# Gate columns moved from the channel-major tiles to the token-major products of a hybrid decoder layer

## The reference

```
h = rmsnorm(x); proj = h @ w_in
u, z, xbc, dt_raw, qk, v, i_raw, f_raw, o_raw = split(proj)      # 512,768,1280,12,768,768,6,6,768
y_a = s5(u):    diagonal complex state space, 32 groups x 16 channels, state 64,
                then g = gelu(y); y_a = g * sigmoid(g @ w_glu + b_glu)
y_b = ssd(z, silu(causal_conv(xbc)), softplus(dt_raw + bias)):  12 heads, gated by silu(z), norm
y_c = mlstm(silu(causal_conv(qk)), v, i_raw + b_i, log_sigmoid(f_raw + b_f)): 6 heads, * sigmoid(o_raw)
x = x + rmsnorm(concat(y_a, y_b, y_c) @ w_out)
x = x + rmsnorm((silu(h2 @ w_gate) * (h2 @ w_up)) @ w_down)      # h2 = rmsnorm(x)
```

## Time and profile before

| | before |
|---|---|
| median of 3 runs | 2898.15 us (2896.5 to 2898.3) |
| profiled execution, its own time | 2895.86 us |
| its span, mean granted clock of TensorE | 2894.0 us, 0.994 |
| PE busy | 2846.0 us (98%) |
| DVE, ACT, POOL busy | 66%, 41%, 13% |
| the 640 + 640 + 640 matmuls of L1900 | 387, 371, 370 ns mean (they overlap) |
| idle of PE before L1900, and what ended most | 5.1 us, DVE t_w_lo L1761 4.3 |
| chain that ended last | PE 47%, DVE 2%, DMA 1%, ACT 1% |

### The profile page before, as it was taken

One profiled execution on the slowest core, in us unless ns is written; L12 is line 12 of the kernel. 1 busy time (PEld: TensorE's weight loads), 2 busy tenths in 40 slices (PEclk: granted clock), 3 DMA queues, 4 the chain that ended last, 5 costly groups with the idle time before them and its releaser, 6 DMA issues.

```text
span 2894.0 us, 36039 instructions
## 1 busy us (share of the span) xinstructions
PE 2846.0 (98%) x13576; PEld 2304.7 (80%) x13576; DVE 1903.5 (66%) x2616; ACT 1191.6 (41%) x2005; POOL 386.0 (13%) x496
## 2 busy tenths in 40 slices
PE   8999999999999989999999999999999999999998
PEld 5888888777777767888888788888888888888887
DVE  7677887666853358887343776666866655656656
ACT  6222222454443445545333533333533333545543
POOL 0000000012530236664121100000000000000000
PEclk9999999999999999999999999999999999999999
DMA  4222443446665958887878654444542223866862
GB/s 162 73 73 86 135 132 112 145 143 203 222 198 159 299 173 279 278 300 272 303 268 332 239 197 164 168 153 165 172 172 94 106 98 138 333 194 210 285 195 103
DMA packets 294569, 545.14 MB, mean 188 GB/s; under 512 B 59228, under 2 KB 150780, under 8 KB 284924
## 3 DMA queue, kind: packets, MB, share of 16 engines
q1 hardware_dynamic: 262636, 437.69, 45.2%
q0 software_dynamic: 24704, 75.52, 6.9%
q10 hardware_dynamic: 7056, 29.63, 2.6%
HBM read 358.30 MB, written 184.44 MB: 188 GB/s over the span
## 4 chain that ended last, share of the span: by engine, by line
PE 47%; DVE 2%; DMA 1%; ACT 1%; issue 1%; SPq 0%; DVEq 0%; ACTq 0%
PE f_banks L2985 25%; PE f_banks L2993 14%; PE f_banks L2087 7%; DMA f_h_raw<-hq 1%; PE f_banks L2290 0%; DMA f_bop2lo<-hq 0%; DVE f_snap L2788 0%; DVE f_w_op L2762 0%; DVE f_a L2800 0%; ACT f_w_op L2624 0%; DVE f_a L2795 0%; ACT o_late L2191 0%; ACT f_snap L2642 0%; DVE f_raw L2776 0%; DVE f_bop2lo L2755 0%
## 5 line engine op out<-in xcount | busy, mean ns | idle before, releaser
L2993 PE MATMUL f_banks<-f_d_op 128*128 128x512 f32 x1848 | 419.0, 389 | 0.0
L2993 PEld LDWEIGHTS f_banks<-f_d_op 128*128 128x128 f32 x1848 | 347.1, 188 | 71.8
L2832 DVE TENSOR_TENSOR f_d_op<-f_d_raw,f_d_op 128x1024 fp32r<-128x1024 f32 x154 | 187.4, 1225 | 149.0 <-ACT f_d_op L2663 148.4
L674 PE MATMUL t_banks<-h_hi,c_w_hi 128*128 128x512 f32 x640 | 254.5, 398 | 0.0
L1900 PE MATMUL t_banks<-t_w_hi,h_hi 128*128 128x512 f32 (+1 forms) x640 | 247.9, 387 | 5.1 <-DVE t_w_lo L1761 4.3
L674 PE MATMUL t_banks<-h_hi,c_w_lo 128*128 128x512 f32 x640 | 250.0, 391 | 0.0
L674 PE MATMUL t_banks<-h_lo,c_w_hi 128*128 128x512 f32 x640 | 249.3, 389 | 0.0
L2663 ACT ACTIVATE f_d_op<-f_d_raw 128x1024 fp32r<-128x1024 f32 x154 | 162.8, 1061 | 198.3 <-PE f_banks L2993 161.5
L1900 PE MATMUL t_banks<-t_w_lo,h_hi 128*128 128x512 f32 (+1 forms) x640 | 237.7, 371 | 0.0
L1900 PE MATMUL t_banks<-t_w_hi,h_lo 128*128 128x512 f32 (+1 forms) x640 | 236.8, 370 | 0.0
L2642 ACT ACTIVATE f_snap<-f_banks 128x1024 f32<-128x1024 f32 x88 | 90.3, 1026 | 253.6 <-PE f_banks L2985 253.6
(11 more groups left out here) (410 smaller groups left out, 6293.3 us busy)
## 6 DMA issues: line engine op xcount, KB each, us to landing
f_raw<-in_w_gu SPq DMA_DIRECT2D x88, 512.0 KB, 6.3
sop<-f_a SPq DMA_DIRECT2D x154, 256.0 KB, 2.0
f_d_raw<-sop SPq DMA_DIRECT2D x154, 256.0 KB, 2.9
t_raw<-in_w_tok SPq DMA_DIRECT2D x72, 512.0 KB, 4.6
f_d_raw<-top SPq DMA_DIRECT2D x88, 256.0 KB, 4.4
m_bc<-rows SPq DMA_DIRECT2D x16, 1152.0 KB, 6.8
f_d_raw<-in_w_dn SPq DMA_DIRECT2D x66, 256.0 KB, 3.1
o_y_lo<-y_lo SPq DMA_DIRECT2D x16, 1024.0 KB, 7.8
```

The lines of the kernel that those rows point to most:

```text
L674: last = nc.tensor.matmul(banks[:, p % RING, :], w[:, n % 2, k, :], h[:, q, k, :], start=k == 0 and j == 0, stop=k == KD - 1 and j == 2)
L2832: tt(d_op[d % D_RING][:, 2:4], d_raw[:, d % S_RING], d_op[d % D_RING][:, 0:2].bitcast(F32), sub).then_inc(dlo_ok, 1)
L2993: last = nc.tensor.matmul(banks[:, bank, :], d_op[d % D_RING][:, s, tok], d_op[d % D_RING][:, w, :], start=k == 0 and j == 0, stop=k == FU ...
```

## The change

- Channel stage: the gate tile is gone (20 tiles, 4 pieces fewer); the convolved tiles begin one tile earlier against the work on S5's constants. ACT does the sines and cosines of that work ahead of an evacuation, not behind it. Tile 8 of the convolved ones (NOT_TOK) is no longer stored token-major: 4 pieces of 4 transposes fewer, and narrower loads in the mixers. Two semaphores become one.
- L707's products alternate between the two lanes, in the order q, r, g. In the S5 steps the input products (L1932) change their loops from lane, r to r, lane.
- Token stage: the 24 gate columns stand ahead of v, z and o; the 2328 columns go in five groups of 466 (the last 464), each of two units with 4 of the 8 depth tiles. The first group (gate columns and 442 of v) is made for all four blocks before the others, with weights that are loaded and split once. 160 slots of 12 matmuls. The weight splits are 68 of 932 columns, before 72 of 1024. One narrow group of each block now begins with 162 columns of Silu and ends with 304 of Sigmoid; another is Copy 326, Silu 140.
- The first 16 evacuations also copy the gate columns to gate_cols; PE transposes them to rows in PSUM (gate_transposes), which DVE's gate work reads. DVE clears gate_cols in the last channel tile.
- POOL sends 7 pieces of a tile per block, before 6. The slots of gates, S5, GLU and mixers are later by 4 to 20, in a list that is longer by 16.

```diff
-    GATE, FIRST = UT, UT + 1
+    FIRST = UT
...
-                evac(n, q)
                 if n == 2 and q == 0:
                     trigonometry()
+                evac(n, q)
...
-                for g in range(2):
-                    lanes = slice(g * S5P, (g + 1) * S5P)
-                    for q in range(2):
-                        for r, b_in in enumerate((bbr, bbi)):
+                for q in range(2):
+                    for r, b_in in enumerate((bbr, bbi)):
+                        for g in range(2):
+                            lanes = slice(g * S5P, (g + 1) * S5P)
...
-    AHEAD, AHEAD_MASK, AHEAD_EXP, AHEAD_W, AHEAD_1 = 112, 129, 132, 116, 140
+    AHEAD, AHEAD_MASK, AHEAD_EXP, AHEAD_W, AHEAD_1 = 132, 148, 151, 136, 156
...
-    WIDTH = (NB, NB, NB, NB, NB // 2)
-    PARTS = (((ACT.Silu, 0, 0, NB),),
-             ((ACT.Silu, 0, NB, NB // 2), (ACT.Copy, NB // 2, XW + VW + NB, NB // 2)),
-             ((ACT.Copy, 0, XW + VW, NB),),
-             ((ACT.Sigmoid, 0, XW, NB),),
-             ((ACT.Sigmoid, 0, XW + NB, NB // 2),))
-    GATE_SLOT, GATE_STEP, COLS = 6, 11, (8, 6, 6, 8)
-    S5_SLOT, S5_STEP = 52, 2
-    GLU_SLOT, GLU_STEP = 90, 14
+    WIDTH = (WT, WT, WT, WT, XW + 2 * VW + GATES_T - 4 * WT)
+    V_AT = XW + VW
+    V0 = WT - GATES_T
+    Z0 = WT - (VW - V0)
+    Z1 = Z0 + WT
+    O0 = WT - (XW - Z1)
+    PARTS = (((ACT.Copy, GATES_T, V_AT, V0),),
+             ((ACT.Copy, 0, V_AT + V0, VW - V0), (ACT.Silu, VW - V0, 0, Z0)),
+             ((ACT.Silu, 0, Z0, WT),),
+             ((ACT.Silu, 0, Z1, XW - Z1), (ACT.Sigmoid, XW - Z1, XW, O0)),
+             ((ACT.Sigmoid, 0, XW + O0, VW - O0),))
+    GATE_SLOT, GATE_STEP, COLS = 10, 12, (8, 6, 6, 8)
+    ROWS_SLOT, ROWS_STEP = 9, 8
+    S5_SLOT, S5_STEP = 61, 2
+    GLU_SLOT, GLU_STEP = 99, 14
...
+                if e < QT * BLK:
+                    nc.scalar.activation(gate_cols[:, e, 0:HS], banks[:, e % QT, 0:HS], ACT.Copy)
+                    nc.scalar.activation(gate_cols[:, e, FR:GCW].rearrange("p (g r) -> p g r", g=2)[:, :, 0:HM],
+                                         banks[:, e % QT, HS:GATES_T].rearrange("p (g r) -> p g r", g=2), ACT.Copy)
...
+                    nc.vector.memset(gate_cols, 0.0)
...
-            b, i = divmod(unit, UNITS_T)
-            return (b * GROUPS_T + i // 2) if i % 2 or i == UNITS_T - 1 else None
+        def group_of(n):
+            return (n, 0) if n < BLK else ((n - BLK) // (GROUPS_T - 1), 1 + (n - BLK) % (GROUPS_T - 1))
+        def weights_of(step_):
+            return step_ % 2 if step_ < 2 * BLK else step_ - 2 * BLK + 2
...
+            def gate_transposes(c):
+                if c == 0:
+                    pe.wait_ge(const_in, 80)
+                    banks_read(pe)
+                pe.wait_ge(evac_ok, QT * (c + 1))
+                if c >= 2:
+                    pe.wait_ge(args_ok, c - 1)
+                for a in range(QT):
+                    last = nc.tensor.transpose(row_banks[c % 2][:, a * P:(a + 1) * P], gate_cols[:, QT * c + a, 0:RG], ident_sb[:])
+                last.then_inc(rows_mm, 1)
...
-                for e in range(2):
-                    lanes = slice(e * S5P, (e + 1) * S5P)
-                    for r in range(2):
+                for r in range(2):
+                    for e in range(2):
+                        lanes = slice(e * S5P, (e + 1) * S5P)
...
-        halves = [w[half, :, :, n * NB:(n + 1) * NB] for n in range(4) for half in range(2)]
-        rest = w[:, :, :, 4 * NB:].reshape(KD, P, NB // 2)
-        return np.stack([unit.transpose(1, 0, 2).reshape(P, -1) for unit in halves + [rest]])
+        w = np.concatenate([w, np.zeros((D, 5 * WT - w.shape[1]), np.float32)], 1)
+        w = w.reshape(2, KD // 2, P, 5, WT)
+        return w.transpose(3, 0, 2, 1, 4).reshape(10, P, KD // 2 * WT)
```

More of the change, by code:

```diff
@@ L1470, in split_at, with row_step @@
         def split_at(slot):
-            unit, t = divmod(slot, 4)
-            both = 4 * unit in range(GATE_SLOT, GATE_SLOT + GATE_STEP * BLK, GATE_STEP)
-            if t > 1 or unit + 1 == UNITS:
-                return ()
-            return (() if t else (0, 1)) if both else (t,)
+            step_, t = divmod(slot, 4)
+            follows = step_ + 1 < STEPS_T and (step_ == 0 or step_ + 1 >= 2 * BLK)
+            return ((weights_of(step_ + 1), t),) if t < 2 and follows else ()
+        def row_step(slot):
+            c, r = divmod(slot - ROWS_SLOT, ROWS_STEP)
+            return c if r == 0 and 0 <= c < BLK else None
         def glu_step(slot):
@@ L1502, in tiles_sent @@
             for b in range(2):
[L1503 removed]
+                eng.wait_ge(out_sent[b], 16 * sends(TILES_T * BLK - TILES_LAST * (BLK - blocks) + b))
         def glu_done(eng):
@@ L1529, in load @@
                     tok_stored(sp)
-                sp.dma_start(raw[half][:], w_tok[unit % UNITS_T, :, half * 2 * NB:(half + 1) * 2 * NB]).then_inc(raw_in[half], 16)
+                sp.dma_start(raw[half][:, 0:2 * WT], w_tok[unit if unit < 2 else 2 + (unit - 2) % W_UNITS, :, half * 2 * WT:(half + 1) * 2 * WT]
+                             ).then_inc(raw_in[half], 16)
             def ahead(q):
@@ L1587, in _ @@
             c_sync(sp, ahead)
-            for unit in range(UNITS):
+            for unit in range(STEPS_T):
                 for t in range(4):
-                    if t < 2 and unit + 2 < UNITS:
-                        load(unit + 2, t)
+                    if t < 2 and unit == 0:
+                        load(2, t)
+                    elif t < 2 and 2 * BLK < unit + 2 < STEPS_T:
+                        load(weights_of(unit + 2), t)
                     slot = 4 * unit + t
@@ L1639, in send_s5 @@
                                    ys[j * S5H:(j + 1) * S5H]).then_inc(y_sent, 16)
-            for unit in range(UNITS):
-                n = group(unit)
+            for unit in range(STEPS_T):
                 for t in range(4):
-                    if n is not None:
-                        send(QT * n + t)
+                    if unit % 2:
+                        send(QT * (unit // 2) + t)
                     q = s5_step(4 * unit + t)
@@ L1665, in upper @@
                     convolved(act, 2 + 2 * unit)
-                nc.scalar.activation(w_hi[unit % 2][half][:], raw[half][:], ACT.Copy).then_inc(whi_ok, 1)
+                nc.scalar.activation(w_hi[unit % 2][half][:, 0:2 * WT], raw[half][:, 0:2 * WT], ACT.Copy).then_inc(whi_ok, 1)
             def ahead(q):
@@ L1730, in _ @@
             c_scalar(act, ahead)
-            for unit in range(UNITS):
-                n = group(unit)
+            for unit in range(STEPS_T):
                 for t in range(4):
                     slot = 4 * unit + t
-                    for half in split_at(slot):
-                        upper(unit + 1, half)
-                    if n is not None:
-                        evac(QT * n + t)
+                    for part in split_at(slot):
+                        upper(*part)
+                    if unit % 2:
+                        evac(QT * (unit // 2) + t)
                     gates(slot)
@@ L1865, in _ @@
             c_vector(dve, ahead)
-            for unit in range(UNITS):
+            for unit in range(STEPS_T):
                 for t in range(4):
                     slot = 4 * unit + t
-                    for half in split_at(slot):
-                        lower(unit + 1, half)
+                    for part in split_at(slot):
+                        lower(*part)
                     gates(slot)
@@ L1967, in _ @@
                     products(unit, t)
+                    c = row_step(slot)
+                    if c is not None:
+                        gate_transposes(c)
                     gates(slot)
```

146 lines of the change are left out of this document (77 added, 69 removed).

## The result

| | before | after |
|---|---|---|
| median | 2896.5 us (5 runs, 2894.96 to 2898.3) | 2911.3 us (5 runs, 2909.05 to 2914.39) |
| profiled span | 2894.0 us | 2907.3 us |
| ratio after/before | | 1.0051, 95% interval 1.0036 to 1.0065 |

The change makes the kernel slower by about 15 us. The forecast was 2893, 5 us faster, with a range of 2870 to 2914: the time lies inside the range, on the other side of no change. A second measurement beside other runs on another chip gives 1.0048 (1.0032 to 1.0064).

A forecast was written before the change was run, and what follows sets the result against it. PE's own columns were taken to set the time (PE 98% busy), other engines showing only where PE stops. Terms from -21.8 to +9 summed to -4.6 us, giving 2893 us, with an 8-in-10 range of 2870 to 2914.

The forecast's parts named there:

- Gate tile, lanes, transposes, channel stall: Channel stage: gate tile -21.8, L707's lanes paired -3.5, tile 8's transposes gone -1.9, PE waiting before first transposes +6.9 us.
- Products: Token-major matmuls: 1920 of 466 or 464 columns, about 207 ns each by a straight line, cost +4.0 us.
- Gates' phase: Token stage: weights split once leave the gates' chains nearly free in early slots, so PE's stalls shrink, -5 us.
- S5 steps: Token stage: PE's work between steps shrinks below DVE's recurrence, so PE waits in each of 15 steps, +3.8 us.
- Group of Silu and Sigmoid: Last block: two table loads a tile make ACT late for a lower, and POOL's mask delays sends, +9 us.
- GLU entry: First GLU product waits for the last g by DMA while the slots before it are shorter, +1.5 us.
- R2: Rival: ACT's tables bind in all four blocks, +21 us, 2914; chance 0.22.
- R3: Rival: 466 columns cost as much as 512, +41.6 in place of +4.0, 2931; chance 0.04.
- R1: Rival: the waits don't come in channel stage, recurrence or ACT's tables; 2867; chance 0.12.
- R4: Rival: L1932 gains too and the gates' stalls go fully, -8 and -5 more, 2880; chance 0.06.
- The drain behind a table load: Skill page's 1.38 us drain beside each 1.28 load, making the two-function group dearer in every block; some 2927; chance 0.02.

The follow-up runs named there:

- e5: Changed kernel with the split weights laid 512 columns apart in place of 466, products still 466 wide: 2909.88 us, 1.0048 against before.
- e3: Changed kernel with S5_SLOT 62 in place of 61, so the S5 steps stand at even slots as before: 2898.55 us, 1.0004 against before.
- e4: Changed kernel with SP's loads for the later S5 steps issued ahead of their slot's weight loads, first two steps' unmoved: 2901.35 us, 1.0012 against before.
- e10: Changed kernel with all S5 loads ahead of their slot's weights, the first two steps' ahead of those of slots 56 and 57: 2901.01 us, 1.0014 against before.
- e1: Changed kernel with Silu in place of Sigmoid in the two-function group, so part of the result differs: 2901.91 us, 1.0013 against before.
- e2: Changed kernel with columns reordered so that no group has both Silu and Sigmoid: 2900.21 us, 1.0009 against before.
- e6: Changed kernel with WT 512: four groups of 512 columns and one of 280 per block: 2943.83 us, 1.0164 against before.

## Why the prediction was wrong

- *Gate tile, lanes, transposes, channel stall*: forecast -20.3 together (-21.8, -3.5, -1.9, +6.9), measured -20.0. (In the other profiles with the same lane order the token stage begins at 508.1 to 510.1, so that number is good to about 1.) Each showed where it was said: stall 5.1, lane groups 0.98, the input products unchanged. Right. One reading in it was wrong and harmless: the window 189.43 to 213.55 holds no L707; four transposes take 0.35 to 0.53 to the next matmul all the same.
- *Products, +4.0*: mis-sized. The spacing of 512 columns was read in the channel stage, 226.7; in the token stage it was 11.02/48 = 229.6 already before, and 466 are 10.16/48 = 211.7, not 207.3. By these spacings the 1920 products take 407 against 398: +8 to +9, where the forecast had +4.0. Most of the rest of the 11.6 is half clock behind the new stalls. e5 shows that alignment isn't the cause. Why the token stage is 3 ns a matmul dearer was not looked into.
- *Gates' phase, -5*: PE's waits there went from 5.9 to 2.6 us, and the half clock after the 3.43 stall is gone. Right in kind and roughly in size.
- *S5 steps, +3.8*: this is the step that failed. It priced DVE's recurrence, and that came about as said (2.1 in thirteen waits). It took the recurrence for all that a step waits for, and left out the loads that SP issues: they are in no sentence of the working. PE's waits for u went from 1.1 to 13.0 us, so the step's waits cost 14.0 more in place of 3.8, with half clock behind them. The move from slot 52 to 61 puts the steps at odd slots, where two weight loads stand ahead of every other step's loads: 6.6, which e3 and e4 take away. The first step's wait, 1.06 before and in no term, became 6.4, and e10 takes it away by the place in the queue alone. That ACT's tables are what makes the queue late there is shown for the issue of the loads (e1, e2) and not for the whole wait. The order of SP's program would have shown the two weight loads.
- *Group of Silu and Sigmoid, +9*: the mechanism is right (two loads a tile, each 1.28), the stall is 4.0, at the lower end of the bounds; the mask did delay sends, but ACT waited only 0.58 and 0.74 for them. What was missed is the same group in the first block, where it delays an upper, the lower behind it and so SP's loads ahead of the first S5 step. Without the double loads the kernel is 10 to 11 us faster (e1, e2), so the term's size of 9 comes near, but by luck: it is not one stall in the last block.
- *GLU entry, +1.5*: measured +1.3 in the profile (1.95 for 0.65); in the other kernels with 466 columns the wait is 1.1 to 3.9.
- *The time*: 2911 lies in the range because the range was wide; the forecast's direction was wrong, 5 faster against 15 slower.
- *Rivals*: R2 (tables bind in more than the last block; 2914) was the nearest: time 2911. But that is luck. It named each block's fourth group as the place; blocks two and three have no such stall, and the first paid through SP. R3 falls (466 columns take 18 ns less than 512). R1 and R4 fall. The drain behind a table load, which the Trainium skill gives ("ScalarE: Activation LUTs", "What ACT_TABLE_LOAD costs"), isn't in these rows either: the load at 659.60 ends at 660.88, and the next activation starts at 660.89. The working's 2927 for it doesn't follow from its own terms: 4 x 8 + 6 over 2893 is 2931.

## What to carry to other kernels

When slots move, walk every queue past the new places, DMA issuers first: a load costs what stands ahead of it, and here an odd slot for an even one was 7 us of waits (7.1 to 0.8 in e3). Don't let one evacuation need two function tables; put a copied range between them in the layout (e2: 11 us). And keep slots equal where the same side work is tied to every slot (e6: 34 us).

## What the runs showed that was not expected

- Matmuls of 512 columns follow at 226.7 ns in the channel stage and at 229.6 in the token stage of the same kernel, on the same clock; 466, 480 and 512 columns there are 211.7, 217.7 and 230.4.
- Removing the first wait for u (5.6 us in e4) gave nothing in e10, as another of 4.6 stood right behind it.
- Asking for u 5 us sooner (e2) shortened the wait by little: 8.1 us from issue to landing in place of 5.5.
- The same program on different chips agrees within 0.05% (2896.5 to 2897.5 for the kernel before), but single executions of the changed kernels lie up to 7 us from their medians.
